# Reciprocal row sums sent through DRAM, and a turn's output finished by ScalarE copies and Pool additions

## The reference, cut to what matters

```python
s = einsum('bhqd,bhkd->bhqk', qb, kh) * scale + cb[..., :, None] - c[..., None, :]   # FoX; memory: no c, no mask
p = softmax(where(mask, s, -inf), axis=-1)
o = einsum('bhqk,bhkd->bhqd', p, vh)
o = o * silu(gate)
```

## Time and profile before

| | us |
|---|---|
| median of 3 runs (lowest, highest) | 1407.98 (1406.86, 1414.48) |
| the profiled execution | 1410.44 |
| its span in the profile | 1408.6 |
| busy: PE, DVE, ACT, POOL | 1281.9, 671.4, 547.2, 416.0 |

### The profile page before, as it was taken

The page is one execution under the profiler, slowest core; times in us unless marked ns, Lnnn a source line. Parts: engine busy times, 40 slices in busy tenths (PEclk is TensorE's granted clock), DMA queues, the critical chain, the costliest instruction groups (busy, mean ns, idle before and its releaser), DMA issues. The chain is left out here.

```text
span 1408.6 us, 20363 instructions
## 1 busy us (share of the span) xinstructions
PE 1281.9 (91%) x6624; PEld 1038.4 (74%) x6624; DVE 671.4 (48%) x1622; ACT 547.2 (39%) x1131; POOL 416.0 (30%) x464
## 2 busy tenths in 40 slices
PE   5898999999999999999976759998999999599997
PEld 4887867888777777788854546786777777478886
DVE  4564414200545544500045547887887888322222
ACT  3563214012222222211145646776777777310100
POOL 5222431021444444430005682223223412300000
PEclk9999999999999999999977888999999999799999
DMA  6454213222544454331156535134341611465453
GB/s 212 150 156 127 76 59 114 74 82 83 157 150 153 149 157 154 125 105 64 46 150 186 133 74 137 51 112 93 89 137 29 154 24 24 146 210 193 180 205 121
DMA packets 118350, 170.40 MB, mean 121 GB/s; under 512 B 11908, under 2 KB 74628, under 8 KB 116404
## 3 DMA queue, kind: packets, MB, share of 16 engines
q1 hardware_dynamic: 115768, 160.65, 37.9%
q10 hardware_dynamic: 2304, 8.39, 1.5%
q0 software_dynamic: 192, 0.33, 0.2%
HBM read 103.19 MB, written 66.13 MB: 120 GB/s over the span
## 5 line engine op out<-in xcount | busy, mean ns | idle before, releaser
L834 PE MATMUL cg_cps<-h_T,tok_slot 128*128 128x512 f32 x2112 | 493.7, 393 | 3.4 <-POOL tok_slot L1074 3.4
L834 PEld LDWEIGHTS cg_cps<-h_T,tok_slot 128*128 128x128 f32 x2112 | 396.4, 189 | 89.2 <-POOL tok_slot L1074 4.3
L1719 PE MATMUL out_yps<-out_w,out_mix 128*128 128x512 f32 x768 | 177.4, 393 | 18.3 <-DMA out_mix<-scr_mix 17.3
L1719 PEld LDWEIGHTS out_yps<-out_w,out_mix 128*128 128x128 f32 x768 | 145.8, 190 | 49.8 <-DMA out_mix<-scr_mix 17.5
L1559 DVE TENSOR_SCALAR_CACHE_REDUCE fox_prob<-fox_sps 128x512 f32<-128x512 f32 (+2 forms) x240 | 142.1, 607 | 37.8 <-PE fox_sps L1444 34.9
L1521 ACT ACTIVATE fox_pT<-fox_tps 128x512 fp32r<-128x512 f32 x240 | 124.6, 531 | 90.1 <-PE fox_tps L1454 87.6
L1570 DVE TENSOR_TENSOR fox_pT<-fox_tps,fox_pT 128x512 fp32r<-128x512 f32 x240 | 141.7, 605 | 21.6 <-ACT fox_pT L1521 20.9
L1454 PE MATMUL fox_tps<-all_ident,fox_prob 128*128 128x128 f32 x816 | 135.1, 278 | 15.4 <-ACT fox_prob L1513 8.5
L1467 PE MATMUL fox_ops<-fox_pT,fox_v 128*128 128x512 f32 x480 | 137.3, 376 | 0.0
L1454 PEld LDWEIGHTS fox_tps<-all_ident,fox_prob 128*128 128x128 f32 x816 | 100.4, 141 | 45.5 <-ACT fox_prob L1513 11.6
L1439 PE MATMUL fox_sps<-fox_ka,fox_qa 128*128 128x512 f32 (+2 forms) x240 | 107.4, 448 | 17.4 <-PEq L1376 14.0
(11 more groups left out here) (187 smaller groups left out, 1676.3 us busy)
## 6 DMA issues: line engine op xcount, KB each, us to landing
scr_split<-cg_stage SPq DMA_DIRECT2D x64, 256.0 KB, 2.8
out_mix<-scr_mix SPq DMA_DIRECT2D x32, 512.0 KB, 4.2
tok_xin<-in_w_cols SPq DMA_DIRECT2D x22, 512.0 KB, 4.4
tok_xin<-in_x SPq DMA_DIRECT2D x16, 512.0 KB, 3.9
scr_gates<-cg_stage SPq DMA_DIRECT2D x32, 256.0 KB, 2.4
out_x<-in_x SPq DMA_DIRECT2D x16, 512.0 KB, 6.1
out<-out_o ACTq DMA_DIRECT2D x16, 512.0 KB, 5.0
scr_fox_v<-tok_vst SPq DMA_DIRECT2D x16, 384.0 KB, 2.9
```

Of the source, the lines that this page charges most:

```text
L834: mm = nc.tensor.matmul(cps[u % 2][:, :], w[j % 2][a_][:, kk, :], hT[b_][:, kk, c * CH:(c + 1) * CH], start=(kk == 0 and r == 0), stop=(kk ...
L1719: mm = nc.tensor.matmul(yps[s][:, c, :], mix[s][a][:, kk, :], w[b][:, kk, c * CH:(c + 1) * CH], start=(kk == 0 and n == 0), stop=(kk == MI ...
```

## The change

The reciprocals go to DRAM and come back broadcast, in place of the products with the identity. ACT stores `rinv` (128 x 4) to a new scratch row of 512 (`store_inverses`), after the first `pt_high` of turn t; SP loads that row into all 64 partitions of `scale` (`load_scale`), for turn t+1 at the start of its iteration t, ahead of the wait for turn t's output; for turn 0 of the stage after all first loads. Both wait for `gate_scaled`, the count of gate products that POOL has done, so that neither the row in DRAM nor `scale` is overwritten too early. `rps` and PE's `spread_sums` are gone, and their PSUM bank is the fourth `tps`.

The upper and the lower half of `ops` are both copied by ACT (`copy_out`, to `o` and `low`, now two buffers of `low`), and POOL adds them; DVE's `add` is gone. POOL has five operations per turn.

```diff
+        self.inv = dram("scr_inv", [2, CH], F32)
...
-        low = k.sb("low", [DH, CH])
+        low = [k.sb(f"low{b}", [DH, CH]) for b in range(2)]
...
-        tps = [k.ps(f"tps{b}", [P, CH]) for b in range(3)]
+        TPS = 4
+        tps = [k.ps(f"tps{b}", [P, CH]) for b in range(TPS)]
...
-        rps = k.ps("rps", [P, CH])
...
+                def load_scale(r, t):
+                    b = t % 2
+                    sp.wait_ge(inv_stored[b], 16 * (r * (n_turns // 2) + t // 2 + 1))
+                    sp.sem_inc(sp_goes, 1)
+                    sp.wait_ge(gate_scaled, r * n_turns + max(t - 1, 0))
+                    sp.sem_inc(sp_goes, 1)
+                    sp.dma_start(scale[b][:, :], scr.inv[b].partition_broadcast(DH)).then_inc(scale_loaded[b], 16)
+
                 def round_(r, last):
                     for t, (e, g) in enumerate(turns):
-
+                        if t + 1 < n_turns:
+                            load_scale(r, t + 1)
+                        elif not last:
+                            load_scale(r + 1, 0)
...
+                load_scale(0, 0)
                 rounds(sp, round_)
...
-                        pe.wait_ge(pt_lo, K.at(n - 2 if n >= 3 else 0))
+                        pe.wait_ge(pt_lo, K.at(max(n - TPS + 1, 0)))
...
-                            pe.wait_ge(added, G.at(max(t - 1, 0)))
+                            pe.wait_ge(copied, 2 * G.at(max(t - 1, 0)))
...
-                    def spread_sums(t):
-
-                        pe.wait_ge(inverted, G.at(t + 1))
-                        pe.wait_ge(scaled, G.at(t))
-                        for i in range(4):
-                            mm = nc.tensor.matmul(rps[0:DH, i * P:(i + 1) * P],
-                                                  rinv[t % 2][:, i:i + 1].to_broadcast([P, DH]), ident[:, :],
-                                                  start=True, stop=True)
-                        mm.then_inc(spread, 1)
...
-                    def low_half(t):
+                    def copy_out(t):
                         act.wait_ge(weighed, K.at(at_turn(t + 1)[1]))
-                        act.wait_ge(added, G.at(t))
-                        nc.scalar.activation(low[:, :], ops[t % 2][DH:P, :], ACT.Copy).then_inc(low_done, 1)
-                        act.wait_ge(spread, G.at(t + 1))
                         act.wait_ge(o_lo, G.at(max(t - 1, 0)))
-                        nc.scalar.activation(scale[t % 2][:, :], rps[0:DH, :], ACT.Copy).then_inc(scaled, 1)
+                        nc.scalar.activation(o[t % 2][:, :], ops[t % 2][0:DH, :], ACT.Copy).then_inc(copied, 1)
+                        nc.scalar.activation(low[t % 2][:, :], ops[t % 2][DH:P, :], ACT.Copy).then_inc(copied, 1)
+
+                    def store_inverses(t):
+                        b = t % 2
+                        act.wait_ge(inverted, G.at(t + 1))
+                        act.sem_inc(act_goes, 1)
+                        act.wait_ge(gate_scaled, G.at(max(t - 1, 0)))
+                        act.sem_inc(act_goes, 1)
+                        act.dma_start(scr.inv[b].rearrange("(i p) -> p i", p=P), rinv[b][:, :],
+                                      allow_slow_non_contiguous=True).then_inc(inv_stored[b], 16)
...
                             pt_high(u, k0 + m)
+                            if m == 0:
+                                store_inverses(t)
...
                         dve.wait_ge(expd, E.at(QT * (t + 1)))
-                        dve.wait_ge(spread, G.at(max(t - 1, 0)))
+                        dve.wait_ge(inv_stored[t % 2], 16 * (r * (n_turns // 2) + t // 2))
...
-                    def add(t):
-                        dve.wait_ge(low_done, G.at(t + 1))
-                        dve.wait_ge(o_lo, G.at(max(t - 1, 0)))
-                        nc.vector.tensor_tensor(o[t % 2][:, :], ops[t % 2][0:DH, :], low[:, :], ALU.add
-                                                ).then_inc(added, 1)
...
-                        pool.wait_ge(scaled, G.at(t + 1))
+                        pool.wait_ge(scale_loaded[b], 16 * (r * (n_turns // 2) + t // 2 + 1))
                         nc.gpsimd.tensor_tensor(gate[b][:, :], scale[b][:, :], gate[b][:, :], ALU.mult
                                                 ).then_inc(gate_scaled, 1)
+                        pool.wait_ge(copied, 2 * G.at(t + 1))
+                        nc.gpsimd.tensor_tensor(o[b][:, :], o[b][:, :], low[b][:, :], ALU.add).then_inc(added, 1)
```

More of the change, by code:

```diff
@@ L1453, in transposes @@
                                 pe.wait_ge(expd, E.at(QT * t + i + 1))
-                            mm = nc.tensor.transpose(tps[n % 3][:, i * P:(i + 1) * P],
+                            mm = nc.tensor.transpose(tps[n % TPS][:, i * P:(i + 1) * P],
                                                      prob[t % 2][:, i, j * P:(j + 1) * P], ident[:, :])
@@ L1496, in round_ @@
                                 weigh(*waiting.pop(0))
-                            if ends(t, m):
-                                spread_sums(t - 1)
                     for x in waiting:
                         weigh(*x)
-                    spread_sums(n_turns - 1)
                 round_(0, False, prologue=True)
@@ L1520, in pt_high @@
                         act.wait_ge(weighed, K.at(max(n - PT + 1, 0)))
-                        nc.scalar.activation(pT[n % PT][HI][:, i0 * P:CH], tps[n % 3][:, i0 * P:CH], ACT.Copy
+                        nc.scalar.activation(pT[n % PT][HI][:, i0 * P:CH], tps[n % TPS][:, i0 * P:CH], ACT.Copy
                                              ).then_inc(pt_hi, 1)
-                    def low_half(t):
+                    def copy_out(t):
                         act.wait_ge(weighed, K.at(at_turn(t + 1)[1]))
-                        act.wait_ge(added, G.at(t))
-                        nc.scalar.activation(low[:, :], ops[t % 2][DH:P, :], ACT.Copy).then_inc(low_done, 1)
-                        act.wait_ge(spread, G.at(t + 1))
                         act.wait_ge(o_lo, G.at(max(t - 1, 0)))
-                        nc.scalar.activation(scale[t % 2][:, :], rps[0:DH, :], ACT.Copy).then_inc(scaled, 1)
+                        nc.scalar.activation(o[t % 2][:, :], ops[t % 2][0:DH, :], ACT.Copy).then_inc(copied, 1)
[8 more added lines that the diff above has]
+                                      allow_slow_non_contiguous=True).then_inc(inv_stored[b], 16)
                     if prologue:
@@ L1542, in round_ @@
                             if ends(t, m):
-                                low_half(t - 1)
-                    low_half(n_turns - 1)
+                                copy_out(t - 1)
+                    copy_out(n_turns - 1)
                 round_(0, False, prologue=True)
@@ L1569, in pt_low @@
                         dve.wait_ge(pt_hi, K.at(n + 1))
-                        nc.vector.tensor_tensor(pT[n % PT][LO][:, i0 * P:CH], tps[n % 3][:, i0 * P:CH],
+                        nc.vector.tensor_tensor(pT[n % PT][LO][:, i0 * P:CH], tps[n % TPS][:, i0 * P:CH],
                                                 pT[n % PT][HI][:, i0 * P:CH].bitcast(F32), ALU.subtract
@@ L1596, in round_ @@
                             pt_low(u, k0 + m)
-                            if ends(t, m):
-                                add(t - 1)
-                    add(n_turns - 1)
                 for head in opening:
```

7 lines of the change are left out of this document (5 added, 2 removed).

## The result

| | us |
|---|---|
| before, median (lowest, highest) | 1408.38 (1406.86, 1414.48) |
| changed, median (lowest, highest) | 1500.06 (1493.49, 1509.99) |
| ratio, 95% interval | 1.065 (1.057 to 1.072) |

What follows compares the result with a forecast made beforehand. POOL was taken to bound the memory attention, PE the forgetting attention. Their terms, +32.7 and -24.9 us, sum to +7.8, which on the median of 1408.0 gives 1415.8 us; the range is 1402 to 1428.

Steps and rivals of the forecast that it cites:

- the price of the store: ACT's store of the reciprocals lands in 4.9 us (bounds 2.5 and 10); 7 us are covered, so nothing is paid.
- Rival A: Slow four-byte stores, 10 us each, make SP wait: +18 in the memory attention, none in the forgetting, about 1433; chance 0.14.
- The memory attention, +32.7: The memory attention grows by 32.7 us (bounds +28 to +37): POOL starts late, has longer turns and two waits.
- the wait at turn 4: In the memory attention POOL waits 7.4 us for the reciprocals' load, queued behind 11 head loads.
- the one at turn 8: In the memory attention POOL waits 3.1 us for the reciprocals' load, queued behind five head loads.
- a turn at 6.29: POOL's fifth operation, the addition, lengthens its memory attention turn from 4.79 to 6.29 us; 16 turns take 100.6 us.
- SP's place: SP loads the reciprocals behind all first loads, so POOL starts the memory attention at 761.1 and not 737.5 us.
- The forgetting attention, -24.9: The forgetting attention shortens by 24.9 us (bounds -19 and -29), mostly through work and waits that PE loses.
- spreads (22.2): In the forgetting attention PE loses four identity products per turn, 1.01 us in 22 turns: 22.2 us saved.
- bank (3.4): In the forgetting attention the fourth transpose bank removes 3.4 of PE's 6.7 us wait for DVE's low half.
- B: Low end everywhere: first broadcast by 757, turn 8's wait gone, PE regains all waits; 1404 to 1408, no change; chance 0.16.
- C: SP's order does not bite: memory attention +10, total -15, 1393; decides if that stage grows under 18 us; chance 0.08.

Runs made afterwards that it cites:

- e2: The changed kernel with four DRAM rows, reciprocal tiles and store semaphores instead of two, so ACT's store waits for the product of turn t-4: 1493.3 us.
- e12: e10 with the bystander's 512 pieces of 4 bytes lying 64 bytes apart in DRAM instead of side by side: 1424.4 us.
- e1: The changed kernel with the reciprocals stored as 16 contiguous bytes per partition, 128 pieces instead of 512 of 4 bytes: 1420.6 us.
- e10: e1 plus a bystander: after each store ACT also stores 512 adjoining pieces of 4 bytes to a DRAM row that nobody reads: 1502.6 us.
- e4: The kernel before with only the addition moved: ACT copies both halves and POOL adds them, PE still spreads the reciprocals: 1423.7 us.
- e17: e15 with SP's loads of the factors moved: turns 0 and 1 before the next stage's first loads, t+2 behind turn t's output stores: 1413.3 us.
- e15: The changed kernel with e1's 16-byte store in both attentions, the order undone by a strided read in POOL's product: 1423.5 us.
- e11: The kernel before in the memory attention, e15's version in the forgetting attention only: 1388.9 us, ratio 0.986 to before.
- e18: e11 with the addition of the two halves on DVE again, ACT copying the low half alone: 1388.8 us, ratio 0.985 to before.
- e9: The changed kernel with 512 pieces of 16 bytes (8 KB) stored instead of 512 of 4 bytes: 1425.6 us.
- e14: e10 with the bystander's 512 pieces of 4 bytes going to an SBUF tile, 64 bytes apart within a partition, not to DRAM: 1423.8 us.
- e8: The changed kernel storing one column of the reciprocals, 128 pieces of 4 bytes instead of 512, with the DRAM rows filled at the start: 1517.5 us.

## Why the prediction was wrong

**The step that failed is the price of the store, twice over.** I estimated its landing at 4.9 us from the mean packet of SP's queue (74 ns) and called the bounds 2.5 and 10; it was 10.3, and 12.6 in e2. e12 gives what the estimate was about, 512 pieces of four bytes: 3.8 us when they lie apart. The mean packet was the wrong row to go by. ACT's queue in part 3 of e1, and then of e10, whose row is also that of e12:

```profile
q10 hardware_dynamic: 8064, 8.47, 1.7%
```
```profile
q10 hardware_dynamic: 29184, 8.56, 2.5%
```

Over spans of 1417.8, 1496.1 and 1422.9 us on 16 engines, the 21120 packets more take about 10 ns each in e10 and 9 in e12, an estimate from rounded shares. So 32 of them on an engine are 0.3 us and not 2.4, close together or not: the delay of the crowded ones does not lie in their own packets' time.

The second half is the graver one: I priced the store only as a latency, paid by the one who waits for it. "Nothing is paid" stood there, and 45 us in the memory attention and 40 in the forgetting attention were. Rival A, at just the 10 us that it names, gave +18 and 1433, and "in the forgetting attention nothing". The bystander shows that the price lies mainly in traffic: e10, whose loop has a store of 6.2 us, below the 7 that A asks for, is as slow as the changed kernel. In the forgetting attention this took back more than the whole gain: 394.7 us against 354.7 in e1 and 379.1 before.

**The memory attention, +32.7.** Right, once that store is out of the way: 32.8 in e1. Its parts answer to e1's timeline of POOL:

```profile
761.72 1.26 POOL L1620 TENSOR_TENSOR att_gate<-att_scale,att_gate 64x512 f32<-64x512 f32 x1 [43.15 <-DMA att_scale<-scr_inv]
...
793.21 1.26 POOL L1620 TENSOR_TENSOR att_gate<-att_scale,att_gate 64x512 f32<-64x512 f32 x1 [6.14 <-DMA att_scale<-scr_inv]
...
824.79 1.26 POOL L1620 TENSOR_TENSOR att_gate<-att_scale,att_gate 64x512 f32<-64x512 f32 x1 [7.35 <-DMA att_scale<-scr_inv]
...
867.34 1.26 POOL L1620 TENSOR_TENSOR att_gate<-att_scale,att_gate 64x512 f32<-64x512 f32 x1
```

The start was forecast at 761.1 and is 761.72; the wait at turn 4 at 7.4 and is 6.14; the one at turn 8 at 3.1 and is 7.35; one of 1.03 at turn 2 was not forecast; a turn at 6.29 and is 6.05. That last term was too large by 0.24 us: the addition does not read the product before it, so POOL starts it 1.22 us after the product and not 1.50. Over 16 turns this is -3.8 us, about what the waits are longer in all. So that the sum is right to 0.1 us is luck: two misses cancel. Its causes are shown by single changes: Pool's fifth operation by e4 (13.8 us, with one more copy on ACT), SP's place by e17 (10.3). The two overlap with the two waits, so they need not add up to 32.8.

**The forgetting attention, -24.9.** Right in e1 (-24.4), e15 (-23.6) and e11 (-23.3). That its gain is the spreads with the bank and not the addition is shown (e4: -0.5, e18); how it divides between spreads (22.2) and bank (3.4) was not tried.

**The rivals.** B and C, the low side: SP's place did bite, as e1's start shows, and even with early loads (e17, where the third turn still waits 18.96 us) the memory attention grows by 25.4 us, more than the 18 up to which C would hold. What C prices, the fifth operation alone, is e4: 13.8 us for its +10. A named the right object and the wrong price. The Trainium skill (DMA: Bandwidth & Descriptors, section Rules for kernel authors) says that a non-contiguous last dimension becomes one descriptor per element, and the profile after agrees. ACT's queue had 2304 packets before; the 21120 more of the changed kernel are 40 stores of 512 + 16:

```profile
q1 hardware_dynamic: 118968, 165.89, 41.5%
q10 hardware_dynamic: 23424, 8.47, 2.3%
```

(The share of SP's own queue rose from 37.9 to 41.5% with the broadcasts' 3200 packets; in e1, with the same packets, it is 39.6%.) But e9 has the same 23424 and is 75 us faster, so their number alone was not what to fear. The Trainium skill (DMA: Bandwidth & Descriptors, section Specifications) says that transfers below 512 B are done by read-modify-write. If that alone were the price, e1, e12 and e14 would be as burdened as the changed kernel; they are not, so by these runs the size below 512 B is not what costs, and the crowding of writes in DRAM is. Whether read-modify-write is what makes the crowded ones wait for each other, no run shows.

Of what I had said would show it, POOL's first product came at 765.86 for 761 and ACT stood still for 28.66 us for 24. The turns were a bound in pairs only, and PE had new waits of more than 5 us in the forgetting attention (18.3 for ACT against 8.5, 25.0 for DVE against 3.2), which I had named as the sign of a wrong forecast.

## What to carry to other kernels

Before small results go through DRAM, ask in which order they lie there: write what a partition holds as one contiguous piece, and undo the order where the data is read on chip. A new kind of transfer has two prices, its own landing and what it does to the transfers beside it; the second is found by a bystander whose data nobody reads. And where one function serves two stages with different limits, read the change for each: here TensorE's four products per turn and their PSUM bank were worth 23 us where TensorE sets the pace, and in the stage where Pool does, the whole change cost 33 even with the fast store.

## What the runs showed of the hardware

- 512 writes of four bytes to 2 KB of DRAM land after 10.3 to 12.6 us (changed kernel, e2) and slow the other queue's transfers of 128 KB in the memory attention from 3.1 to 10.0 and from 2.5 to 7.1 us (e10 against e1); spread 64 bytes apart they land after 3.8 and slow these transfers by 0.4 at most (e12). The cost rises with the writes per 64 bytes of DRAM (16: 82 us for 40 stores, 8: 27, 4: 5 to 12, 1: 4), and with their number: a quarter of the crowded writes costs an estimated 51 us (e8).
- A small packet takes about 10 ns of its DMA engine, crowded (e10) or not (e12: 9), an estimate from part 3; the delay of the crowded ones is not in it.
- A read in Pool's product of 64x512 float32 with a stride of 16 bytes takes 1.55 us for 1.28:

```profile
L1980 POOL TENSOR_TENSOR fox_gate<-fox_scale,fox_gate x24: 1506/1554/1637, 869.2 to 1182.4; 64x512 f32<-64x512 f32 x24
```

- Where PE was starved, its granted clock was lower, as a mean between its two levels of 1.2 and 2.4 GHz: over 784 to 830 us it was 0.96 before, with PE busy 41.8 of 46 us, 0.69 in the changed kernel (19.8 busy), and still 0.72 in e1 (25.5), where POOL sets the pace.
